# Folding the squares of four norms on VectorE before TensorE sums them, and spreading inverse roots with transposes

## The reference, cut to what matters

```python
def rmsnorm(x, g):
    xf = x.astype(jnp.float32)
    y = xf * lax.rsqrt(jnp.mean(xf * xf, axis=-1, keepdims=True) + EPS)
    return (y * g.astype(jnp.float32)).astype(x.dtype)
```

## Time and profile before

| | |
|---|---|
| median of 3 runs | 1071.0 us (1068.98 to 1071.57) |
| profiled execution, its own time | 1074.56 us |
| its span in the trace | 1072.8 us |
| mean granted TensorE clock | 0.978 of full |
| TensorE matmul busy | 1044.9 us (97%) |
| VectorE busy | 679.7 us (63%) |
| ScalarE busy | 586.6 us (55%) |
| HBM over the span | 182 GB/s |

### The profile page before, as it was taken

How to read it: one execution, slowest core, us unless ns; L and a number is a source line. 1 busy time by engine, 2 the same in 40 slices (tenths; PEclk the granted TensorE clock), 3 DMA queues, 4 the chain that set the end, 5 groups by cost and what they waited for, 6 DMA issues and landing times.

```text
span 1072.8 us, 19928 instructions
## 1 busy us (share of the span) xinstructions
PE 1044.9 (97%) x8394; PEld 1009.5 (94%) x8394; DVE 679.7 (63%) x1134; ACT 586.6 (55%) x965; POOL 0.4 (0%) x5
## 2 busy tenths in 40 slices
PE   7999899999999999999999999999999999999997
PEld 5699799999999999999989999999999899999996
DVE  7576777858887676776726655555676547554542
ACT  4679765646655555666725535445566546443442
POOL 0000000000000000000000000000000000000000
PEclk9999999998999999899989999999999999999998
DMA  9665566633666454353313645545553426454511
GB/s 383 268 255 207 208 230 242 216 154 124 236 270 226 167 187 170 155 203 125 145 40 133 258 166 191 192 166 187 202 197 122 153 80 252 181 197 169 185 40 40
DMA packets 27880, 196.42 MB, mean 183 GB/s; under 512 B 3088, under 2 KB 3728, under 8 KB 4496
## 3 DMA queue, kind: packets, MB, share of 16 engines
q1 hardware_dynamic: 26928, 194.16, 48.3%
q10 hardware_dynamic: 864, 0.98, 0.3%
HBM read 194.09 MB, written 1.05 MB: 182 GB/s over the span
## 4 chain that ended last, share of the span: by engine, by line
PE 85%; DVE 6%; ACT 6%; issue 1%; DMA 1%; SPq 0%; DVEq 0%; ACTq 0%
PE PS L833 21%; PE PS L835 21%; PE PS L834 21%; PE PS L954 4%; PE PS L955 3%; PE PS L957 3%; DVE wlo L1510 2%; PE PS L988 1%; PE PS L1108 1%; ACT whi L1175 1%; PE PS L990 1%; PE PS L989 1%; PE PS L842 1%; DMA raw<-wada 1%; PE PS L1130 1%
## 5 line engine op out<-in xcount | busy, mean ns | idle before, releaser
L1510 DVE TENSOR_TENSOR wlo<-raw,whi 128x1024 fp32r<-128x1024 f32 (+1 forms) x314 | 367.5, 1217 | 133.5 <-ACT whi L1175 133.3
L1175 ACT ACTIVATE whi<-raw 128x1024 fp32r<-128x1024 f32 (+1 forms) x314 | 311.9, 1046 | 173.1 <-PE PS L835 173.1
L833 PE MATMUL PS<-Hh,whi 128*128 128x256 f32 x1200 | 343.9, 287 | 2.3 <-ACT V L1347 2.3
L835 PE MATMUL PS<-Hh,wlo 128*128 128x256 f32 x1200 | 340.9, 284 | 0.0
L834 PE MATMUL PS<-Hl,whi 128*128 128x256 f32 x1200 | 340.9, 284 | 0.0
L833 PEld LDWEIGHTS PS<-Hh,whi 128*128 128x128 f32 x1200 | 231.7, 193 | 5.7 <-issue 2.8
L833 PE MATMUL PS<-Oh,whi 128*128 128x256 f32 x816 | 231.3, 284 | 0.8 <-DVE Ol L1490 0.7
L834 PEld LDWEIGHTS PS<-Hl,whi 128*128 128x128 f32 x1200 | 231.7, 193 | 0.2
L835 PEld LDWEIGHTS PS<-Hh,wlo 128*128 128x128 f32 x1200 | 231.7, 193 | 0.0
L834 PE MATMUL PS<-Ol,whi 128*128 128x256 f32 x816 | 230.9, 283 | 0.0
L835 PE MATMUL PS<-Oh,wlo 128*128 128x256 f32 x816 | 230.9, 283 | 0.0
(11 more groups left out here) (231 smaller groups left out, 1224.9 us busy)
## 6 DMA issues: line engine op xcount, KB each, us to landing
raw<-wall SPq DMA_DIRECT2D x155, 1024.0 KB, 4.9
raw<-wada SPq DMA_DIRECT2D x18, 1024.0 KB, 4.9
GA<-wada SPq DMA_DIRECT2D x2, 1024.0 KB, 26.3
GA<-alibi SPq DMA_DIRECT2D x1, 2048.0 KB, 9.2
raw<-wall SPq DMA_DIRECT2D x2, 768.0 KB, 6.1
X<-xt SPq DMA_DIRECT2D x1, 1024.0 KB, 5.5
KM<-wada SPq DMA_DIRECT2D x1, 1024.0 KB, 16.0
QF<-wada SPq DMA_DIRECT2D x1, 1024.0 KB, 19.3
```

Of the source, the lines that this page charges most:

```text
L833: e.matmul(dst, wh, a, start=start, stop=False, skip_group_check=share)
L835: return e.matmul(dst, wl, a, start=False, stop=stop, skip_group_check=share)
L1175: e.activation(whi[place(n)][:, c], raw[i % RAW][:, c], ACT.Copy).then_inc(*up("a_whi", (n, half)))
L1510: e.tensor_tensor(wlo[place(n)][:, c], raw[i % RAW][:, c], f32(whi[place(n)][:, c]), ALU.subtract).then_inc(*up("v_wlo", (n, half)))
```

## The change

Two things. `spread` issues a transpose of the repeated column instead of a matmul with the identity; it makes 36 blocks of 128x128 in all (2 for each of eight norms, 4 for `a0`, 4 for each of the four groups of heads). And for `a0`, `a1`, `m0`, `m1` DVE adds the squares of g = 3 too, then the two halves of the accumulator to each other, so that `total` sums one tile instead of four; for `a0`, `sum2` is folded to one tile in the same way.

```diff
@@ constants
+    FOLDED = ("a0", "a1", "m0", "m1")
@@ tensor: spread
-                m = e.matmul(
-                    PS[:, b, c0 + 128 * h:c0 + 128 * h + 128], src[:, h:h + 1].to_broadcast([128, 128]), ID[:, :],
-                    start=True, stop=True)
+                m = e.transpose(
+                    PS[:, b, c0 + 128 * h:c0 + 128 * h + 128], src[:, h:h + 1].to_broadcast([128, 128]), ID[:, :])
@@ tensor: step total
+                elif name in FOLDED:
+                    on.wait_ge("v_sq", (name, "folded"))
+                    sums(b, 0, [SQ[:, 2, :]], name)
+                    if name == "a0":
+                        on.wait_ge("v_sq", ("final", "folded"))
+                        sums(b, 2, [sum2[:, 0:T]], "both")
                 else:
...
                     on.wait_ge("v_sq", (name, 2))
                     sums(b, 0, [SQ[:, 2, :], SQ[:, 3, :], last_squares, SQ[:, 1, :]], name)
-                    if name == "a0":
-                        on.wait_ge("v_sq", ("final", 3))
-                        sums(b, 2, [sum2[:, 0:T], sum2[:, T:2 * T]], "both")
@@ vector: step square
+                elif g == 3 and name in FOLDED:
+                    on.wait_ge("a_sq", (name, 3))
+                    e.tensor_tensor(pair(SQ, 2), pair(SQ, 2), pair(SQ, 0), ALU.add).then_inc(*up("v_sq", (name, 3)))
+                    on.wait_ge("v_sq", (name, 3))
+                    e.tensor_tensor(SQ[:, 2, :], SQ[:, 2, :], SQ[:, 3, :], ALU.add).then_inc(*up("v_sq", (name, "folded")))
@@ vector: step final_squares
+                if i == 3:
+                    on.wait_ge("v_sq", ("final", 3))
+                    e.tensor_tensor(sum2[:, 0:T], sum2[:, 0:T], sum2[:, T:2 * T], ALU.add).then_inc(
+                        *up("v_sq", ("final", "folded")))
```

## The result

| | changed kernel | kernel before | ratio, 95% interval |
|---|---|---|---|
| first comparison | 1061.12 us (1060.27 to 1062.96, 4 runs) | 1070.93 us (1068.98 to 1071.57, 4 runs) | 0.9909 [0.9887, 0.9931] |
| again, in the second set of experiments | 1062.1 us (1060.43 to 1065.77, 6 runs) | 1070.79 us (1065.84 to 1073.31, 17 runs) | 0.9929 [0.9910, 0.9947] |

The change gains 9.7 us (7.4 to 12.1) by the first comparison and 7.6 us (5.7 to 9.6) by the second. The forecast was 6.5 us. The time lies in the forecast range and on the forecast side, and the size was too small.

The account below looks back on a forecast made before the run. TensorE, busy 97% of the span, was taken as the bound. Spreads 3.7 us and folds 2.7 us, together given as 6.5 us, off the 1071.0 us median gave 1064.5 us, range 1060.5 to 1068.0 us.

Parts of the forecast that it names:

- The spreads: On TensorE, a block's transpose takes one record where the matmul took two, 0.22 to 0.11 us: 3.7 us gained in all.
- `ffn` and `end`: Two spread blocks each, serial and at half clock: two fewer records give 0.43 us at each norm, 0.85 us together.
- The spreads of `q` and `kv`: Counted as no gain, since ScalarE paces what follows until about 120 us; at most 0.44 us.
- The folds at `m0` and `a1`: 16 records of sums become 4, folded tile ready 1.1 and 0.45 us before TensorE arrives: 1.26 us gained each.
- VectorE's wait ahead of the reciprocal: At the folded norms the additions lie in VectorE's existing wait, so it shortens by some 2 us each, weights not delayed.
- The fold at `m1`: TensorE waits 1.0 us for the folded tile, then needs 4 records: gain 0 to 0.4 us, taken as 0.2 us.
- The fold at `a0`: 24 records of sums become 8, but TensorE waits for VectorE's additions, 1.9 and 0.7 us: gain 0.
- I expect the low stretch at `a0` to stay and no new one to come.: TensorE's 6.8 us at the lower clock level from 446 to 460 us, costing 3.4 us, stays; no other appears.
- Rival 1: The lower-clock stretch at `a0` vanishes or shortens: at most 3.4 us more gained, likely 2.7, 1061.8 us; chance 0.10.
- Rival 2: VectorE swallows some early spread gains and one more lower-clock stretch costs 3.4 us: around 1068 us; chance 0.12.
- Rival 3: The transpose in `spread` still costs two records, leaving only the folds' 2.7 us: 1068.3 us; chance 0.05.
- Rival 4: Transposes let the clock fall after norms and head groups, 3.4 us per new stretch: slower, 1074.7 us; chance 0.03.

Follow-up runs that it names:

- before_shifted: The kernel before with 8 unneeded matmuls (1.77 us) inserted ahead of the first block's output projection: 1068.23 us, ratio 0.9993 to the kernel before.
- whole_again: The changed kernel, unaltered, timed again beside the kernel before: 1062.10 us, ratio 0.9929.
- shifted: The changed kernel with 8 unneeded matmuls (1.77 us) inserted ahead of the first block's output projection: 1067.70 us, ratio 0.9969 to the kernel before.
- spread_only: The kernel before with transposes in `spread` and no folding: 1065.58 us, ratio 0.9961 to the kernel before.
- covered_folds: The changed kernel with folds only at `m0` and `a1`, `a0` and `m1` summing as before: 1061.24 us, ratio 0.9921 to the kernel before.

## Why the prediction was right, and where it fell short

- **The spreads, 3.7 us.** Right. One record for a block, 0.11 us each: 0.44 us for four. The part alone measured 4.2 us (2.8 to 5.6). At `ffn` and `end`, two blocks move the chain by 0.70 us for 1.24 us. There the forecast had 0.43 us each and 0.54 us came. The spreads of `q` and `kv`, costed at nothing, are worth nothing: with the old ones (before_shifted) and with the new (the changed kernel) TensorE leaves the part paced by ScalarE 56.05 us behind the sums of `q`, and the stage takes 172.3 us with both.
- **The folds at `m0` and `a1`, 1.26 us each.** Right: 1.34 us in the clean stage, with 1.2 and 0.5 us to spare (foretold 1.1 and 0.45). VectorE's wait ahead of the reciprocal fell by 2.5 us at `m0` and `a1` and by 1.35 us at `m1`, foretold as some 2 us each. No stage behind them shows late weights.
- **The fold at `m1`, 0.2 us.** Right: a wait of 0.95 us (foretold 1.0) and 0.15 us gained.
- **The fold at `a0`, 0 us.** Right within 0.3 us, on the wrong side. The first wait was 1.91 us as foretold; the second was 0.39 us, not 0.7. In six executions against three it is a loss of 0.3 us.
- **"I expect the low stretch at `a0` to stay and no new one to come."** This step failed. It took the place and length of all low stretches of one trace as fixed, and looked for a change at `a0` alone. The profiled pair has 13.6 us less low time, and the runs with inserted matmuls show that it moves with edits far away and between executions of one program. Of the 7.8 us of the pair that were not foretold, some 5 lie in the three places above and 2.8 in the stage ahead of `ffn`, where one low stretch of the kernel before is absent after and another falls where ScalarE paces. The forecast read the low stretches from the slowest execution of the kernel before (clock 0.978, where its 58 timed runs have 0.983 in the mean).
- **Rival 1**, the stretch at `a0` shorter, came true in part: 3.4 us for 6.8. Its time, 1061.8 us, is nearest to the measured one, though by changes at `ffn` and in the head groups as well. That the median is so near to it is luck: 2.7 us by the clock would need a mean clock 0.0025 higher, and in the timed runs of whole_again it is 0.0006 higher (0.9835 for 0.9829).
- **Rival 2**, one more low stretch, is what shifted looks like: 1067.7 us by 1.77 us of work that has to do with no norm. The price of 3.4 us for a new stretch was that of the 6.8 us at `a0`. Most stretches seen last 3.4 us and cost half of that: the one that whole_again has at 566 us made its stage 1.5 us longer.
- **Rival 3**, two records for a transpose, is refuted by the 36 records.
- **Rival 4**, the transposes let the clock fall, is not borne out. Behind every head group and norm there are transposes now, and low time fell from 34.0 to 20.4 us, in spread_only too; in its timed runs the mean clock is 0.984, for 0.983 in the kernel before. The rule of the Trainium skill ("TensorE: Matmul & The Clock Gate", section "Part 4: PE-mode transpose"), by which a transpose does not count as busy in the way a matmul does, would have lengthened it; no run here shows that, at no more than seven transposes in a row (four of L851 and three of L1112 at 489.58 us).

Why the changed kernel and covered_folds measured above the sum of their steps: the granted clock of the timed runs accounts for it in covered_folds (8.5 us by its ratio, 6.1 us with half the low time taken off, 6.2 us by its steps). For the whole it takes less away, 7.1 us for 7.6, and what is left above the sum is within its error. Open: the first comparison, 9.7 us, since the clock is not on record for its runs of the kernel before, and what sets the places and lengths of the low stretches.

## What to carry to other kernels

Price an instruction by what it moves the chain, and fold on another engine only where the folded tile is ready before TensorE arrives; there this was right to 0.1 us, and elsewhere the fold only turned work into waiting. Where the clock falls in short stretches, a median of a few runs can carry 2 to 4 us that belong to no edit: read the granted clock of every timed run beside its time, compare stages free of such stretches, and run the old and the new kernel once more with some idle work inserted, before a difference of that size is credited to a change.

## What was not expected of the hardware

- 1.77 us of inserted matmuls moved the median of the changed kernel by 4.3 to 5.6 us, 3.55 us of them moved it by about 3 us, and 1.77 us in the kernel before by -0.7 us. What goes beyond the slots is clock: its mean over the timed runs was 0.981, 0.984 and 0.985, for 0.984 in whole_again and 0.982 in the kernel before. In profiles, low stretches between 60 and 1045 us sum to 17.0 to 34.0 us over 14 executions of nearly the same program, and two executions of the same one gave 20.4 and 23.8 us. The Trainium skill says in "TensorE: Matmul & The Clock Gate", section "Part 1: The HAM clock gate (the "warmup" mystery)", that the same kernel shows varying numbers of slow matmuls from run to run, since the change of clock is not tied to the kernel's start. The trace agrees, and adds that edits far away shift it too.
- A stretch of TensorE that holds only one-column sums, 2.1 us of them at `q` and `kv` with no idle time in the rows, can be followed by a low stretch (it begins at 62 to 65 us in 7 of 14 executions).
- Time at the lower level costs half of itself only where TensorE sets the pace: 3.4 us of it at 112 to 116 us, under ScalarE's work, cost nothing, and 3.4 us at 118 to 122 us cost 1.4 us.
- Quiet time as such does not fix it: with TensorE away from its products for 3.6 us at `a0`, it stood at the lower level for 3.4 us behind that in both executions of the changed kernel and for 6.8 us in shifted.
